# Moving weight loads, a weight split, a transposition and a store within the pipelined attention steps of a two-layer trunk

## The reference

```python
def stick_breaking_layer(h, norm_gain, w_in, q_gain, k_gain, w_out):
    u = rms_norm(h, norm_gain)
    proj = u @ w_in
    q, k, v, gate = jnp.split(proj, 4, axis=-1)
    q = rms_norm(split_heads(q, SB_HEADS), q_gain)
    k = rms_norm(split_heads(k, SB_HEADS), k_gain)
    v = split_heads(v, SB_HEADS)
    o = merge_heads(stick_breaking_attention(q, k, v))
    return (o * jax.nn.silu(gate)) @ w_out

def stick_breaking_attention(q, k, v):
    """A[t,s] = beta_ts * prod_{s<j<t}(1-beta_tj), s<t."""
    ...
        z = jnp.einsum('bhtd,bhsd->bhts', qb, kb).astype(jnp.float32) * scale
        ...
        log_beta = jax.nn.log_sigmoid(z)
        log_skip_j = jnp.where(causal, jax.nn.log_sigmoid(-z), 0.0)
        log_skip = lax.cumsum(log_skip_j, axis=3, reverse=True) - log_skip_j
        weights = jnp.where(causal, jnp.exp(log_beta + log_skip), 0.0)
        outs.append(jnp.einsum('bhts,bhsd->bhtd', weights.astype(vb.dtype), vb))
```

## Time and profile before

| | |
|---|---|
| median of three runs | 1176.85 us (1174.12 to 1177.07) |
| the profiled execution's own time | 1174.98 us |
| its span | 1173.3 us |
| TensorE busy | 1145.6 us, 98% |
| VectorE busy | 831.4 us, 71% |
| ScalarE busy | 419.7 us, 36% |
| GpSimd busy | 162.5 us, 14% |
| granted TensorE clock | 1.0 of full speed |

### The profile page before, as it was taken

How to read it: one execution, slowest core, us unless ns; L and a number is a source line. 1 busy time by engine, 2 the same in 40 slices (tenths; PEclk the granted TensorE clock), 3 DMA queues, 4 the chain that set the end, 5 groups by cost and what they waited for, 6 DMA issues and landing times. The chain is left out here.

```text
span 1173.3 us, 19984 instructions
## 1 busy us (share of the span) xinstructions
PE 1145.6 (98%) x7012; PEld 1048.3 (89%) x7012; DVE 831.4 (71%) x1636; ACT 419.7 (36%) x887; POOL 162.5 (14%) x344
## 2 busy tenths in 40 slices
PE   8999999898999999999999999999999999999998
PEld 8999989898988989888888989898999999999787
DVE  5768786858687775774444778788888888788421
ACT  5554454444444444452222222323232322222200
POOL 2413131213122231110003100000000000000000
PEclk9999999999999999999999999999999999999999
DMA  8243545455454531066632110314242421107441
GB/s 251 56 120 113 172 145 183 154 149 185 145 173 136 153 99 46 1 237 209 208 108 72 55 37 19 115 67 137 74 141 71 135 84 45 46 37 292 153 139 72
DMA packets 145214, 141.78 MB, mean 121 GB/s; under 512 B 19936, under 2 KB 117472, under 8 KB 145120
## 3 DMA queue, kind: packets, MB, share of 16 engines
q1 hardware_dynamic: 106336, 120.88, 31.5%
q10 hardware_dynamic: 38784, 19.67, 6.2%
HBM read 93.86 MB, written 46.66 MB: 120 GB/s over the span
## 5 line engine op out<-in xcount | busy, mean ns | idle before, releaser
L28 PE MATMUL p_proj<-w_qkv_hi,ut_hi 128*128 128x384 f32 x504 | 171.9, 341 | 0.4 <-DVE ut_lo L911 0.4
L30 PE MATMUL p_proj<-w_qkv_hi,ut_lo 128*128 128x384 f32 x504 | 169.0, 335 | 0.0
L29 PE MATMUL p_proj<-w_qkv_lo,ut_hi 128*128 128x384 f32 x504 | 168.8, 335 | 0.0
L28 PE MATMUL p_proj<-w_ig_hi,next_hi 128*128 128x256 f32 x512 | 145.5, 284 | 0.0
L29 PE MATMUL p_proj<-w_ig_lo,next_hi 128*128 128x256 f32 x512 | 143.1, 279 | 0.0
L30 PE MATMUL p_proj<-w_ig_hi,next_lo 128*128 128x256 f32 x512 | 143.0, 279 | 0.0
L28 PE MATMUL p_proj<-next_hi,w_qf_hi 128*128 128x512 f32 x282 | 113.2, 401 | 0.0
L923 DVE TENSOR_TENSOR_SCAN a_skip<-a_skip,a_diagonal 128x641 f32<-128x641 f32 (+3 forms) x64 | 86.7, 1355 | 35.1 <-ACT a_beta L742 30.5
L30 PE MATMUL p_proj<-next_hi,w_qf_lo 128*128 128x512 f32 x282 | 110.1, 390 | 0.0
L29 PE MATMUL p_proj<-next_lo,w_qf_hi 128*128 128x512 f32 x282 | 109.9, 390 | 0.0
L28 PEld LDWEIGHTS p_proj<-w_ig_hi,next_hi 128*128 128x128 f32 x512 | 96.2, 188 | 0.0
(11 more groups left out here) (258 smaller groups left out, 2790.3 us busy)
## 6 DMA issues: line engine op xcount, KB each, us to landing
stage<-in_hg_w_in_dram SPq DMA_DIRECT2D x32, 512.0 KB, 4.6
stage<-in_sb_w_in_dram ACTq DMA_DIRECT2D x24, 512.0 KB, 5.3
w_out_hi_scratch<-m_in SPq DMA_DIRECT2D x32, 256.0 KB, 2.1
w_out_lo_scratch<-m_in SPq DMA_DIRECT2D x32, 256.0 KB, 2.5
m_in<-mixed_scratch SPq DMA_DIRECT2D x12, 448.0 KB, 6.0
a_gated<-in_x_dram SPq DMA_DIRECT2D x8, 512.0 KB, 3.9
m_in<-in_sb_w_out_dram SPq DMA_DIRECT2D x16, 256.0 KB, 3.4
ut_hi<-w_out_hi_scratch SPq DMA_DIRECT2D x8, 512.0 KB, 8.1
```

The costliest lines, as they stand in the source:

```text
L28: pe.matmul(out, w_hi, m_hi, start=start, stop=False, skip_group_check=True)
L29: pe.matmul(out, w_hi, m_lo, start=False, stop=False, skip_group_check=True)
L30: return pe.matmul(out, w_lo, m_hi, start=False, stop=stop, skip_group_check=True)
```

## The change

It moves five things in layer 0.

1. On ScalarE, the three loads at the end of a PLAIN step go ahead of the second gate sigmoid, as they are in the FIRST plan.
2. The low parts of the output weights in steps 1 to 4 are made by GpSimd, behind its key multiply of the tiles 0, 1, 5 and 6, and no longer by VectorE: sixteen operations of 128x512.
3. `turn_qk` of the PLAIN steps stands behind the fifth triplet of its place (TURN_AT = 5), not the second.
4. The store of the previous head's outputs stands behind map 4 (STORE_AT = 4), not map 0.
5. SyncE's loop over the steps is written out. The wait for all stored parts of a step stands behind the second read of map 7, ahead of the loads of the next halves; it stood between the two reads.

```diff
-def split_half_lo(dve, m_in, link, group, j):
+def split_half_lo(eng, m_in, link, group, j):
...
+    TURN_AT = 5
+    STORE_AT = 4
...
-            def carry(h, k, group):
+            def carry(h, k):
...
                 for c in range(2):
-                    if c == 1 and group is not None:
-                        for i in range(2):
-                            sp.wait_ge(link["w_parts_stored"][i], group * 64 + 64)
                     read_flipped(sp, h, k, c)
 
-            def carry_all(h, b, group, previous=None):
-
-                if group is not None:
-                    for i in range(2):
-                        load_raw_half(sp, m_in, w_out, link, group, i)
-                for j in range(TILES):
-                    carry(h, j, group if j == TILES - 1 else None)
-                    if j == 0 and previous is not None:
-                        store(previous, 1 - b)
-                    if group is not None and j in SPLITS_AFTER:
-                        what, part = SPLITS_AFTER[j]
+            def carry_all(h, b):
+
+                group = h - 1
+                for k in range(TILES):
+                    carry(h, k)
+                    if k == STORE_AT and h >= 1:
+                        store(h - 1, 1 - b)
+                    if 0 <= group < 4 and k in SPLITS_AFTER:
+                        what, part = SPLITS_AFTER[k]
                         if what == "load":
                             load_raw_half(sp, m_in, w_out, link, group, part)
                         else:
                             store_half(sp, m_in, w_out, link, group, part)
+                if 0 <= group < 4:
+                    for i in range(2):
+                        sp.wait_ge(link["w_parts_stored"][i], group * 64 + 64)
+                if group + 1 < 4:
+                    for i in range(2):
+                        load_raw_half(sp, m_in, w_out, link, group + 1, i)
...
-            carry_all(0, 0, None)
-            with sp.Fori(0, 2) as pair:
-                for b in (1, 0):
-                    carry_all(pair * 2 + 2 - b, b, pair * 2 + 1 - b, pair * 2 + 1 - b)
-            carry_all(HEADS - 3, 1, None, HEADS - 4)
+            for h in range(CARRIED):
+                carry_all(h, h % 2)
...
                     if plan is FIRST and i == USES - 1:
                         for p in range(3):
                             load(2, p)
+                    if plan is PLAIN and i == USES - 1 and not (isinstance(h, int) and h == HEADS - 3):
+                        for p in range(3):
+                            load(h + 3, p)
...
-                    if plan is PLAIN and i == USES - 1 and not (isinstance(h, int) and h == HEADS - 3):
-                        for p in range(3):
-                            load(h + 3, p)
...
-                    if splits_rows(h) and i in SPLIT_AT:
-                        split_half_lo(dve, m_in, link, h - 1, SPLIT_AT.index(i))
...
                     pool.tensor_tensor(raw[i % 4][:, 1, :], raw[i % 4][:, 1, :], rms[:, 1:2].to_broadcast([P, P]),
                                        ALU.mult).then_inc(k_ready, 1)
+                    if splits_rows(h) and i in SPLIT_AT:
+                        split_half_lo(pool, m_in, link, h - 1, SPLIT_AT.index(i))
...
-                            if i >= 3 and i % 2 == 1 and kt == (KT - 2 if plan is SQUEEZED and i == 9 else 2):
+                            if i >= 3 and i % 2 == 1 and kt == (KT - 2 if plan is SQUEEZED and i == 9 else
+                                                            TURN_AT if plan is PLAIN else 2):
                                 turn_qk(h, (i - 3) // 2, plan)
```

More of the change, by code:

```diff
@@ L279, in split_half_hi @@
                    ACT.Copy).then_inc(link["w_hi_made"], 1)
-def split_half_lo(dve, m_in, link, group, j):
+def split_half_lo(eng, m_in, link, group, j):
     _, cols = split_rows(j)
-    dve.wait_ge(link["w_hi_made"], group * 4 + j + 1)
-    dve.tensor_tensor(flat(m_in[0])[:, cols].bitcast(F32R), flat(m_in[0])[:, cols], flat(m_in[1])[:, cols],
+    eng.wait_ge(link["w_hi_made"], group * 4 + j + 1)
+    eng.tensor_tensor(flat(m_in[0])[:, cols].bitcast(F32R), flat(m_in[0])[:, cols], flat(m_in[1])[:, cols],
                       ALU.subtract).then_inc(link["w_lo_made"], 1)
```

## The result

The changed kernel is slower: 1182.06 us (1181.09 to 1184.88) against 1176.85 us, a ratio of 1.0041 with a 95% interval of [1.0028, 1.0054]. I had said 1171.5 us, with a range of 1166 to 1177.5.

A forecast was written before the change was run, and what follows sets the result against it. TensorE, busy 98% of the span, was taken as the bound. Steps 1 to 5 (-0.52, -1.09, +0.39, -3.19, -0.7) sum to -5.1 us, giving 1170 to 1172; forecast 1171.5 us, range 1166 to 1177.5.

The forecast's parts named there:

- `hi1` - S: Varying part of a step, 17.94 to 22.48 us: first score matmul (S) to start of second map's high copy (`hi1`).
- the rest: From `hi1` to the next step's first score matmul: 43.3 us, claimed constant because TensorE has fixed work left.
- Turn later: turn_qk three triplets later in four tiles of each step: directly nothing; its 4.6 us wait returns ahead of L973.
- The low part on GpSimd: GpSimd's split in steps 1 to 4: 1.04 us each, costing VectorE's product and transposition 0.42 (bounds 0, 1.04).
- C: Rival, chance 0.12: GpSimd's split is long and holds SyncE's store of the second map; slower, 1181 us at T = 3.
- T: Time that GpSimd's split takes; the second map's store is held by T - 1.04 us in four steps.
- fronts: First score matmul to VectorE's product for the second map; 10.15 us forecast in steps 1, 2 and 4.
- backs: VectorE's product for the second map to that map's high copy; 9.15 us forecast in steps 1 to 4.
- Loads: Earlier first scan; with the subtraction off VectorE, fronts gain 0.57, 0.92 and 0.93 us in steps 1, 2 and 4.
- Mixed store later: Second map lands sooner without the store's 512 KB; step 4's back -2.26 us, step 5 -0.7 with its front.
- the cap of 12.9 us: Largest gain, if the other steps ran `hi1` - S like step 0: the sum of the differences.
- Rival D: Chance 0.10: later turn delays the loads, the gate sigmoid waits for them, fronts unchanged; gain -2 us, within the bound.

The follow-up runs named there:

- e1: Changed kernel with only the turn put back behind the second triplet (TURN_AT = 2): 1176.57 us, ratio 0.9992.
- e2: Kernel before with only the turn of the six plain steps put behind the fifth triplet: 1182.29 us, ratio 1.0039.
- e4: Changed kernel with the low parts of the output weights back on VectorE: 1172.27 us, ratio 0.9960.
- e9: Kernel before with only the three weight loads ahead of the last gate sigmoid in plain steps: 1168.72 us, ratio 0.9942.
- e8: Kernel before with only the low parts of the output weights moved to GpSimd: 1178.80 us, ratio 1.0016.
- e10: Kernel before with only the mixed outputs' store behind the fifth map instead of the first: 1172.56 us, ratio 0.9972.
- e5: Changed kernel with the turn put back and the low parts back on VectorE: 1168.15 us, ratio 0.9926.
- e7: Changed kernel with five identity transpositions on TensorE between the fourth map's high part and low part, ahead of the second outputs: 1179.59 us, ratio 1.0023.
- e13: Changed kernel with 14 identity transpositions on TensorE ahead of the second outputs, right behind the projection's last matmul: 1177.33 us, ratio 0.9994.

## Why the prediction was wrong

**What bounds the kernel.** Right as a reading of the kernel before: the six steps do add up as (`hi1` - S) and the rest. Wrong in calling the rest constant. It was constant in a trace whose clock never fell, and I took that for a property of the work. (Rows 2 count the wait for the turn four times, not nine as I wrote; no sum hangs on it.)

**Turn later: the step that failed.** I wrote "Directly: nothing", because a wait saved at the turn comes back in front of L973. It did come back: no turn wait, and 18.4 us for L973 where the two had been 16.8. But two waits with 3.8 us of work between them (step 1 of e1) are not the same as one of their sum. The clock fell to 1.2 GHz behind the joined wait, at about 1.56 us each time on the mean, five times in the trace. By the ratios the edit costs 4.6 us alone (e2) and 5.8 in the changed kernel (e1). No rival had this mechanism, and none of the rows before could price it, but the question what the clock does behind a wait half as long again as any in the trace was there to be asked.

**The low part on GpSimd: mis-sized.** I took 1.04 us for the split and 0.42 for what it costs the product. Undisturbed it is 1.28 us; beside VectorE it took 2.0 and 2.7. Where it came first it held the product for 0.74 us (1.86 against 1.12); where it came second it kept SyncE's queue, itself held in step 1 and begun late in step 3. I had seen that "each tenth by which the split is longer than 1.04 goes into the path", and that is what happened. Of the rivals C came nearest: its sum is 0 at T = 2.3, and with splits of 1.3 to 2.7 us fronts and backs together gained 0.56 us. That its price of 1181 us for T = 3 lies next to the measured time is luck, since the clock, which C leaves out, made up the difference. The rule of the Trainium skill's page SBUF — State Buffer, section Who interferes with whom, which I had weighed and set aside for the 0.16 us of rows 5, was right: the product and the split each stand nearly still while the other has the pair (in step 2 the product still took 0.81 us behind the split's end, of 0.96 undisturbed), and the transposition, which has one input, took 0.98 us beside the split as without it.

**Backs.** 9.15 expected in steps 1 to 4; 9.56, 9.81, 9.93 and 9.60 measured, all by the split: with it back on VectorE they are 7.93 to 8.17 (e4). Giving back "about half" of the landing's excess was too cautious.

**Fronts.** Right: 10.15 expected, 10.18, 10.40 and 10.39 measured, and in step 3 +0.53 instead of +0.15. The reason was half right: the loads alone bring the fronts of steps 1, 2 and 4 there (10.18 in e9), and so nearly does taking the subtraction off VectorE alone (10.18, 10.48 and 10.24 in e8); the two together give no more.

**Loads: mis-sized.** From the fronts I had about 2.5 us for them; alone they bring 6.8 (e9). What I left out is that the backs shrink with them, in e9's trace by as much as the fronts. An earlier first map gives SyncE the time for its other stores before the second map is flipped; in step 4 the trace shows that, elsewhere it is my reading.

**Mixed store later.** The place is right (e10: -3.3 us). Step 4's excess, of which it was to take 2.26, is mostly not its doing: that back fell from 11.41 to 10.37 in e10 and to 9.53 in e9, with the store in its old place. The -0.7 that I gave step 5 does not come out of its terms, which make -0.43 and a little; measured is -0.59.

**Step 0.** I had no change there. Its back was 8.12 us before and 9.36 after. In the thirteen traces of the experiments it is 8.05 once (e10) and 9.2 to 9.6 otherwise, in kernels whose step 0 is that of before as well (e8). So it is not the change's. That the profiled execution of before was a lucky one in that place is my reading, and I don't know what sets it; the cap of 12.9 us rested on it.

**Rival D.** It was there in small part: with the later turn the loads came so late that the gate sigmoid at the end of step 3 waited 2.35 us for them, but step 4's front is 10.39 all the same. At the loop's head my reason for step 3 was wrong. VectorE's last operation ahead of the jump ended 1.22 us behind S in the kernel before, in the changed kernel and in e5 alike; the wait behind the jump was 4.56, 5.69 and 3.55 us. What sets that wait stays open.

## What to carry to other kernels

Before moving work out from between two waits of TensorE, ask where the idle time will then lie and not only how much it is in sum; work that costs nothing may be what holds the clock. An edit judged by where its wait goes should be judged together with the others: the same split costs 1.9 us in one surrounding and 7.8 in another, because it took the slack that loads and mixed store had just made. And where an operand comes in parts, start the matmuls that need only the early part.

## What the runs showed of the hardware

- Granted clock: 0.50 behind waits of 2.57 to 3.23 us in the changed kernel, 1.00 behind every wait of the kernel before (up to 1.7 us) in the profiled execution. The length alone does not settle it: 2.54 us in e2 and 2.64 in e4 left it up, and 1.75 us in e8, or 1.65 and 0.56 with work of 0.77 us between them in e7, brought it down. Each fall cost about 1.56 us on the mean. The Trainium skill's page TensorE: Matmul & The Clock Gate, section What's actually happening, says that the throttled clock is the state at rest and that activity lifts it; e13 agrees, where 14 matmuls without use won 5.5 us.
- The kernel before loses its clock too in some executions: of 92 timed beside the experiments the 44 with a mean granted clock of 1.000 have a median of 1175.6 us, the 13 with 0.996 or 0.997 one of 1179.6. So part of the spread between executions goes with the clock.
- GpSimd and VectorE hold each other up on two-input operations whichever starts first: 128x512 on GpSimd takes 1.28 us undisturbed and 2.0 to 2.7 where a scan or a product had begun before it, and the product of 1.12 us took 1.86.
